# One attention stage for prompt and sample in layer 0, and sample keys transposed by VectorE from a re-laid transfer

## What is computed

```
layer 0:  qa,ka,va (8 heads of 64, forgetting attention), qb,kb,vb (4 heads of 2x64, differential attention)
  prompt: causal attention over its 512 tokens
  sample: for each of 8 requests: K, V = cache[page_table[b]] (1024 x 1024 each) + 8 new rows
          softmax(q K^T * scale + forget sums), differential: p1 - lambda * p2, then P V
          the differential half is RMS-normed over 128 ("subln")
  then w_out, residual, SwiGLU
layer 1:  16 query heads, 4 kv heads of 64; an indexer keeps the top keys of each query
  prompt: attention over the selected keys (a mask)
  sample: for each of 8 requests: K, V = cache[page_table[b]] (1024 x 256 each) + 8 new rows, masked
  then w_out, residual, SwiGLU
```

## Time and profile before

| | us |
|---|---|
| median of 3 runs (2239.94 to 2246.65) | 2245.98 |
| the profiled execution | 2245.45 |
| its span, first to last instruction | 2243.7 |
| layer 0: forget sums | 283 to 298.7 |
| layer 0: prompt attention | 298.7 to 400 |
| layer 0: sample attention, with the prompt's subln | 400 to 631.4 |
| layer 0: the sample's subln | 631.4 to 638.2 |
| layer 1: prompt attention with the top keys | 1426 to 1585.8 |
| layer 1: sample attention | 1585.8 to 1709 |

### The profile page before, as it was taken

The page is one execution under the profiler, slowest core; times in us unless marked ns, Lnnn a source line. Parts: engine busy times, 40 slices in busy tenths (PEclk is TensorE's granted clock), DMA queues, the critical chain, the costliest instruction groups (busy, mean ns, idle before and its releaser), DMA issues. The chain is left out here.

```text
span 2243.7 us, 30894 instructions
## 1 busy us (share of the span) xinstructions
PE 1873.8 (84%) x11782; PEld 1460.6 (65%) x11790; DVE 989.5 (44%) x1686; ACT 569.3 (25%) x1051; POOL 138.0 (6%) x111
## 2 busy tenths in 40 slices
PE   3997678488878999999979768566688899999998
PEld 2765445255556997799767543243445699879986
DVE  3436357644433322232234657999343423132312
ACT  2312135233322321122222222233122322112210
POOL 0423002000000000000001320000000000000000
PEclk9998879799988999999999865688788899999999
DMA  4231100499822231223213300000354222223221
GB/s 151 71 103 47 53 10 1 144 381 344 317 79 66 75 94 66 75 81 88 66 52 114 80 0 4 7 1 1 102 153 113 66 75 75 71 79 86 75 71 57
DMA packets 176270, 201.57 MB, mean 90 GB/s; under 512 B 21290, under 2 KB 130666, under 8 KB 176170
## 3 DMA queue, kind: packets, MB, share of 16 engines
q1 hardware_dynamic: 169176, 193.55, 27.3%
q10 hardware_dynamic: 6914, 6.45, 0.9%
q0 software_dynamic: 80, 0.26, 0.0%
HBM read 191.01 MB, written 9.22 MB: 89 GB/s over the span
## 5 line engine op out<-in xcount | busy, mean ns | idle before, releaser
L206 PE MATMUL ps<-feat_lo,w_hi 128*128 128x288 f32 (+1 forms) x1424 | 422.2, 297 | 15.3 <-PEq L436 8.6
L188 DVE TENSOR_TENSOR w_lo<-w_raw,w_hi 128x2048 fp32r<-128x2048 f32 x97 | 222.4, 2293 | 466.4 <-ACT w_hi L182 466.4
L208 PE MATMUL ps<-feat_hi,w_hi 128*128 128x288 f32 (+1 forms) x1424 | 422.3, 297 | 0.0
L207 PE MATMUL ps<-feat_hi,w_lo 128*128 128x288 f32 (+1 forms) x1424 | 421.9, 296 | 0.0
L182 ACT ACTIVATE w_hi<-w_raw 128x2048 fp32r<-128x2048 f32 x97 | 185.5, 1913 | 448.8 <-PE ps L208 415.4
L206 PEld LDWEIGHTS ps<-feat_lo,w_hi 128*128 128x128 f32 (+1 forms) x1424 | 267.5, 188 | 18.3 <-issue 9.1
L208 PEld LDWEIGHTS ps<-feat_hi,w_hi 128*128 128x128 f32 (+1 forms) x1424 | 267.3, 188 | 1.2
L207 PEld LDWEIGHTS ps<-feat_hi,w_lo 128*128 128x128 f32 (+1 forms) x1424 | 267.4, 188 | 1.1
L206 PE MATMUL ps<-w_lo,feat_hi 128*128 128x512 f32 (+2 forms) x560 | 228.5, 408 | 12.6 <-DVE feat_lo L1439 9.5
L207 PE MATMUL ps<-w_hi,feat_lo 128*128 128x512 f32 (+2 forms) x560 | 223.9, 400 | 0.0
L208 PE MATMUL ps<-w_hi,feat_hi 128*128 128x512 f32 (+2 forms) x560 | 222.9, 398 | 0.0
(11 more groups left out here) (236 smaller groups left out, 2299.1 us busy)
## 6 DMA issues: line engine op xcount, KB each, us to landing
s_kslot<-in_cache_l_k_dram SPq DMA_DIRECT2D x64, 512.0 KB, 7.9
s_vslot<-in_cache_l_v_dram SPq DMA_DIRECT2D x64, 512.0 KB, 7.4
w_raw<-in_w_gate_dram SPq DMA_DIRECT2D x44, 512.0 KB, 4.0
w_raw<-in_w_up_dram SPq DMA_DIRECT2D x44, 512.0 KB, 5.2
w_raw<-in_w_in_dram SPq DMA_DIRECT2D x18, 1024.0 KB, 5.2
w_raw<-in_w_down_dram SPq DMA_DIRECT2D x16, 1024.0 KB, 5.1
s_kslot<-in_cache_l_k_dram SPq DMA_DIRECT2D x64, 128.0 KB, 2.2
s_vslot<-in_cache_l_v_dram SPq DMA_DIRECT2D x64, 128.0 KB, 2.7
```

Of the source, the lines that this page charges most:

```text
L188: dve.tensor_tensor(self.K.w_lo[:, n % 2, :], self.K.w_raw[:, n % 2, :], self.K.w_hi[:, n % 2, :].bitcast(F32), ALU.subtract).then_inc(sel ...
L206: pe.matmul(out, lhs[0], rhs[1], start=start, stop=False)
L207: pe.matmul(out, lhs[1], rhs[0], start=False, stop=False)
L208: return pe.matmul(out, lhs[0], rhs[0], start=False, stop=stop)
```

## The change

- **Layer 0**: prompt attention, sample attention and both sublns become one stage, `attend`. The prompt's units, now in 36 steps (32 units and 4 to drain), are run between the parts of each sample batch: two steps, one, one, and what is left of the batch's share of 4 or 5. The differential pairs come first.
- **Prompt attention** (both layers) is a class, `PromptAttention`. One pair of PSUM banks for scores instead of two, so that scores(u) wait for the exponentials of u-1; one bank for transposed probabilities instead of two; both copies out of it on ScalarE; two buffers of probabilities instead of three. The norms are made once per pair from the sums, not per unit; GpSimd no longer scales.
- **Sample attention** (both layers) is a class, `SampleAttention`, with all 8 batches written out. A page of keys comes in 4 DMAs of 32 partitions each, whose source runs are a quarter row (1 KB in layer 0, 256 bytes in layer 1), and VectorE transposes the page in 32x32 blocks in one instruction of 128 x 1024 (layer 0) or 128 x 256 (layer 1). TensorE's 512 + 128 transposes of keys and their 128 + 32 copies out of PSUM go. Query and probability columns are ordered to suit. The page ids are read once for the keys and again for the values, each just before its page's DMAs.
- Layer 0's key slots are a ring of 4 pages, laid in `resid`, which is loaded again at the end of the stage; the value slots lie in `w_hi` and `w_lo`. Layer 1's are tiles of their own, with 8 pages.
- The first 4 pages of keys and of values of layer 0 are issued in `forget_sums`, ahead of its stores.
- Layer 1 runs `prompt_alone` and then `attend` with no prompt.

The diff, cut to its core:

```diff
 def forget_sums
         @block.sync
         def _(sp):
+            sample.load_k(sp, 0, range(sample.loaded_k))
+            sample.load_v(sp, 0, range(sample.loaded_v))
             sp.wait_ge(S["out"], 1)
...
-def prompt_attention(nc, K, tag, q_at, k_at, v_at, gates, mask, mixed, sample_top=None):
+class PromptAttention:
...
+    def tensor(self, pe, x):
+        def scores(u):
+            if u >= 1:
+                pe.wait_ge(S["exped"], 2 * u)
...
+        def turn(u):
+            for i in self.heads_of(u):
+                if self.mixed(p):
+                    pe.wait_ge(S["blended"], self.n_mixed[u + 1])
+                else:
+                    pe.wait_ge(S["exped"], 2 * u + 1 + i)
+                self.bank_free(pe, ("turn", u, i))
+                for j in range(qt + 1):
+                    ins = pe.transpose(self.T[:, j * P:(j + 1) * P], self.probs[:, u % 2, i, j * P:(j + 1) * P],
+                                       K.c("ident"))
+                ins.then_inc(S["turned"], 1)
...
+        if x < n:
+            scores(x)
+        if 1 <= x <= n:
+            turn(x - 1)
+        if 2 <= x <= n + 1:
+            weigh(x - 2)
...
+    def scalar(self, act, x):
+        if 1 <= x <= n:
+            u = x - 1
+            for i in self.heads_of(u):
+                self.bank_filled(act, ("turn", u, i))
+                if u >= 2:
+                    act.wait_ge(S["weighed"], u - 1)
+                act.activation(self.probs_t[:, u % 2, i, 0:self.width(u)], self.T[:, 0:self.width(u)], ACT.Copy)\
+                   .then_inc(S["t_free"], 1)
+        if x < n:
+            act.wait_ge(S["shifted"], x + 1)
...
-def sample_attention(nc, K, tag, cache_k, cache_v, new_v, row_bias, bias_sel, width, chunks, fill_q, new_k, new_mask,
-                     coef, out, subln=None):
+class SampleAttention:
+    BIAS_AHEAD = N_PAGES // 2
...
+    def load_k(self, sp, b, pages):
+        for j in pages:
+            n = b * N_PAGES + j
+            if j == self.BIAS_AHEAD:
+                if b >= 1:
+                    sp.wait_ge(S["scored"], 3 * b)
+                sp.dma_start(self.bias[:, :], self.row_bias(b)).then_inc(S["bias_in"], 16)
+            if n >= self.ring:
+                sp.wait_ge(S["k_turned"], n - self.ring + 1)
+            page = sp.value_load(self.K.pages[0:1, n:n + 1], min_val=0, max_val=self.cache_k.shape[0] - 1)
+            src = self.cache_k[ds(page, 1), :, :].rearrange("z (c i) (a e) -> z a i c e", c=4, a=4)
+            for a in range(4):
+                dst = self.kslot[32 * a:32 * a + 32, n % self.ring, :].rearrange("i (c e) -> i c e", c=4)
+                sp.dma_start(dst, src[0, a]).then_inc(self.k_in[n % self.ring], 16)
+
+    def load_v(self, sp, b, pages):
+        for j in pages:
+            n = b * N_PAGES + j
+            if j == 0:
+                if b >= 1:
+                    sp.wait_ge(S["weighed"], b)
+                sp.dma_start(self.vnew[:, :], self.new_v(b)).then_inc(S["new_v_in"], 16)
+            page = sp.value_load(self.K.pages[0:1, n:n + 1], min_val=0, max_val=self.cache_v.shape[0] - 1)
+            sp.dma_start(self.vslot[:, j, :], self.cache_v[ds(page, 1), :, :].rearrange("a k d -> (a k) d"))\
+              .then_inc(self.v_in[j], 16)
...
+    def turn_k(self, dve, b, pages):
+        for j in pages:
+            n, g = b * N_PAGES + j, j // 4
+            dve.wait_ge(self.k_in[n % self.ring], 64 * (n // self.ring + 1))
+            if b >= 1:
+                dve.wait_ge(S["scored"], 3 * (b - 1) + 1 + g)
+            src = self.kslot[:, n % self.ring, :].rearrange("p (c b i) -> p c b i", c=4, i=32)
+            dst = self.kt[g][:, :, j % 4 * P:(j % 4 + 1) * P].rearrange("p b (c i) -> p c b i", c=4)
+            dve.transpose(dst, src).then_inc(S["k_turned"], 1)
...
+def attend(nc, K, prompt, sample, subln=None, after=None):
+    def gap(b, g):
+        lo, hi = prompt.steps * b // DEC_BATCH, prompt.steps * (b + 1) // DEC_BATCH
+        cuts = (lo, lo + 2, lo + 3, lo + 4, hi)
+        return range(cuts[g], cuts[g + 1])
...
+        def _(sp):
+            sample.load_k(sp, 0, range(sample.loaded_k, N_PAGES))
+            for b in B:
+                sample.load_v(sp, b, range(sample.loaded_v if b == 0 else 0, N_PAGES))
+                if b + 1 < DEC_BATCH:
+                    sample.load_k(sp, b + 1, range(N_PAGES))
+            if after is not None:
...
+                W.load_up_to(sp, after + 1)
+                sp.dma_start(K.resid[:, 0:PT, :], K.x_prompt[0].rearrange("(t p) d -> p t d", p=P)).then_inc(resid_in, 16)
...
+        def _(pe):
+            for b in B:
+                sample.scores(pe, b)
+                prompt_steps(b, 0)
+                sample.turn_probs(pe, b, 0)
+                prompt_steps(b, 1)
+                sample.turn_probs(pe, b, 1)
+                sample.weigh(pe, b)
+                prompt_steps(b, 2)
+                sample.turn_o(pe, b)
+                prompt_steps(b, 3)
...
+        def _(dve):
+            sample.turn_k(dve, 0, range(N_PAGES))
+            for b in B:
+                sample.shift(dve, s, b)
+                prompt_steps(b, 0)
+                if b + 1 < DEC_BATCH:
+                    sample.queries(dve, s, b + 1)
+                prompt_steps(b, 1)
+                sample.new_probs_out(dve, s, b)
+                if b + 1 < DEC_BATCH:
+                    sample.turn_k(dve, b + 1, range(0, 4))
+                sample.o_out(dve, s, b)
+                prompt_steps(b, 2)
+                if b + 1 < DEC_BATCH:
+                    sample.turn_k(dve, b + 1, range(4, N_PAGES))
+                sample.finish(dve, b)
+                prompt_steps(b, 3)
...
 def two_layers
+            sample.loaded_k, sample.loaded_v = 4, 4
+            forget_sums(nc, K, sample)
...
+            attend(nc, K, prompt, sample, SampleSubln(nc, K, pr, K.c("step")), out0[0][0][0])
...
+            sample.loaded_k, sample.loaded_v = 0, 0
+            attend(nc, K, None, sample)
```

More of the change, by code:

```diff
@@ L169, in load_up_to @@
     def load_up_to(self, sp, last):
-        while self.issued <= min(last, len(self.tiles) - 1):
+        while self.issued <= min(last, self.known() - 1):
             n = self.issued
@@ L816, in turn @@
-            def turn(u):
-                p, qt = units[u]
-                for i in range(1 if mixed(p) else 2):
-                    if mixed(p):
-                        pe.wait_ge(S["blended"], n_mixed[u + 1])
-                    else:
-                        pe.wait_ge(S["exped"], 2 * u + 1 + i)
-                    before = u if i == 0 else n_plain[u]
-                    if before >= 1:
-                        pe.wait_ge(out[i], before)
-                    for j in range(qt + 1):
-                        ins = pe.transpose(K.ps[:, 4 + i, j * P:(j + 1) * P], probs[:, u % 3, i, j * P:(j + 1) * P],
-                                           K.c("ident"))
-                    ins.then_inc(turned[i], 1)
@@ L882, in _ @@
-            for x in range(n + 3):
-                if x < n:
-                    exps(x)
-                if 2 <= x < n + 2:
-                    turn_out(x - 2)
-                if x >= 3:
-                    finish(x - 3)
-        if any(mixed(p) for p in range(PAIRS)):
+            for x in range(prompt.steps):
+                prompt.scalar(act, x)
+        @block.vector
+        def _(dve):
+            s, top = Steps(dve, prompt.S["chain"]), Steps(dve, sample_top.chain)
+            for x in range(prompt.steps):
+                prompt.vector(dve, s, x)
+                for i in range(SampleTop.HALVES * x // prompt.steps, SampleTop.HALVES * (x + 1) // prompt.steps):
+                    sample_top.half(dve, top, i)
@@ L900, in _ @@
         @block.vector
         def _(dve):
-            s = Steps(dve, S["chain"])
-            def top(u):
-                dve.wait_ge(S["scored"], u + 1)
-                a = 2 * (u % 2)
-                dve.tensor_reduce(minus[:, 2 * u:2 * u + 2], K.ps[:, a:a + 2, 0:width(u)], AX, ALU.max, negate=True)\
-                   .then_inc(S["shifted"], 1)
-                if sample_top is not None:
-                    for i in range(SampleTop.HALVES * u // n, SampleTop.HALVES * (u + 1) // n):
-                        sample_top.half(dve, s, i)
@@ L940, in finish @@
-            def finish(u):
-                p, qt = units[u]
-                if not mixed(p) and qt == PT - 1:
-                    dve.wait_ge(S["weighed"], u + 1)
-                    dve.tensor_copy(K.att[:, p, 0:SEQ], O).then_inc(S["chain"], 1)
-                    s.n += 1
-                    s.wait()
-                    dve.tensor_tensor(K.att[:, p, 0:SEQ], K.att[:, p, 0:SEQ], R, ALU.mult).then_inc(S["finished"], 1)
-            top(0)
-            for x in range(n + 3):
-                if x + 1 < n:
-                    top(x + 1)
-                if x >= 3:
-                    finish(x - 3)
-                if x < n:
-                    sums(x)
-                if 2 <= x < n + 2:
```

(19 more changed lines are left out.)

1033 lines of the change are left out of this document (495 added, 538 removed).

## The result

The changed kernel takes 2426.5 us (median of 4 runs, 2423.2 to 2432.1) against 2243.8 (4 runs, 2239.9 to 2246.7): ratio 1.0818, 95% interval 1.079 to 1.0846. It is slower by 183 us; 2432 was predicted. The profiled execution has a span of 2425.0 us against 2243.7. One run further down, the one with early turns, had a lower granted clock in the untouched stages too (0.745 over its span against 0.839 in the changed kernel), so its total is not set against the others.

The account below looks back on a forecast made before the run. Layer 1's sample attention was taken as bound by SyncE issuing, layer 0 by a chain of 41 us a batch. 2245.45 + 2 (layer 0) + 15 (layer 1 prompt) + 170 (layer 1 sample) = 2432 us; range 2320 to 2500.

Parts of the forecast that it names:

- all three terms of the sum: Changes added to the profiled 2245.45 us: +2 layer 0, +15 layer 1's prompt attention, +170 layer 1's sample attention.
- SyncE's issues bound layer 1's sample stage: Layer 1's sample attention: SyncE's issuing sets a batch at 35.6 us, the stage 293 against 123.2, +170.
- The bracket: Layer 1's sample attention: low and high SyncE time per batch, 27.6 to 39.6 us around 35.6.
- The rival of cheap issues: Copies into 32 partitions issue in 0.333 us: layer 1 +106, layer 0 -21, total 2345; chance 0.20.
- Layer 1's prompt stage: Layer 1's prompt attention: 175 us with steps of 5.0 us, +15 (-15 to +40).
- fill, drain and the end of the top keys: Layer 1's prompt attention: 9 us for fill, drain and pair ends, 4 for top keys ending with the last step.
- the closed ring: Layer 1's prompt step: scores(x) wait for the exponentials of x-1, those of x behind both copies of x-1; 5.0 us.
- the chain of a batch: Layer 0, from N to next N: transpose, issues of pages 4 to 7, landing, scores, exponentials, prompt steps; 41 us.
- The predicted +2: Layer 0's attention stage: ends at 640 against 638.2 us, +2 (-45 to +28).
- The tail: Layer 0, behind the last N: weighing 4.3, output, first w_out tile's split, the sample's subln; 12 us.
- The reload of x: End of layer 0's stage: with two w_out tiles issued some 15 us before the last batch ends; uncovered, 12 us.
- N: Layer 0: the point in a batch where VectorE has turned out the new probabilities; batches are counted from N to N.

Follow-up runs that it names:

- early turns: Changed kernel, layer 0: VectorE turns the next batch's first four key pages right after the next queries, ahead of prompt steps; 2523.1 us, period 43.3 us.
- Id reads: Changed kernel, layer 1: a batch's eight page ids read once in a row for keys and values; 2394.0 us, sample stage 227.5 us against 265.2.
- copy count: Changed kernel, layer 1: each key page in one copy of 128 rows instead of four; 2348.7 us, sample stage 199.1 us against 265.2.
- the old function: Changed kernel with layer 1's sample attention and its query and key layout from the kernel before; 2281.3 us, that stage 123.3 us.
- without any copies: Changed kernel, layer 0: no key or value page copied in from the second batch on; 2413.1 us, period 41.9 us.
- the prompt first: Changed kernel, layer 0: all prompt steps run in the first gap of batch 0; 2489.0 us, stage 432.6 us.

## Why the prediction was right

The total was 6 us off and its sign and main term were right, but all three terms of the sum were off in size, and two of them rested on a wrong mechanism.

- **SyncE's issues bound layer 1's sample stage: right.** Id reads, copy count and the old function each moved the stage as that says, and SyncE waited 0.5 us. The sizes were high: a copy's pitch is 0.50 us, not 0.60, and an id read 0.58, not 0.75. Batch 31.6 instead of 35.6, the stage +142 instead of +170. The bracket (27.6 to 39.6) held both. The pieces give 8 x 2.58 + 8 x 1.09 + 2 x 0.74 = 30.8 (the bias and vnew at 0.74 each by the timeline above). Most of what is left are the rare long issues: by the key copies alone, 4.4 us over seven batches.
- **The rival of cheap issues was half right:** the instruction is 0.317, like those into 128 partitions, but a written-out copy has two register steps before it, so the pitch is no 0.43.
- **Layer 1's prompt stage: near in size (+21 for +15), the wrong term.** I took the step as 5.0 us before and after and put the growth into fill, drain and the end of the top keys (9 + 4). The 5.0 of before was the whole stage over 32 and held the ends too; the step was 4.58 there and is 5.24 now, and the ends are about as long as they were (18 and 19 us). So the closed ring itself cost 20 us, and that the terms of the ends gave nearly as much was luck. Nor had I counted the clock: 0.73 after, 0.80 before, with TensorE's busy time at 121 us instead of 108 for the same instructions.
- **Layer 0: near in size, wrong in cause.** The step that failed is "VectorE transposes page 0 and so frees a ring slot; SyncE issues pages 4 to 7; the last copy lands", taken as the chain of a batch. SyncE does wait 83.5 us for the turns, but without any copies the period is 41.9, and with early turns 43.3. What remains is TensorE's own list: the prompt's steps and the sample's pieces stand in one in-order queue, and TensorE is busy 260 of 355.6 us at a clock of 0.72 (264 of 332.7 at 0.88 and 0.92 before). A batch has 230.9 / 7 = 33.0 us of it, where the prediction put some 25. (The chain's terms add up to 36.6 and 42.2, not 36.7 and 42.3, which changes nothing.) That these waits in line, with the lower clock, are what makes up the 41.9 was argued from what the two runs leave over; no run opened the rings in layer 0, since all eight banks are in use there.
- **Where layer 0's gain went.** By the run with the prompt first: the new pieces one behind the other take 432.6 us, the old ones 339.5, so the pieces became 93 us longer (steps of 4.9 us for units of 101.3 / 32 = 3.2, and batches of 31.3, the length of SyncE's list, where the reciprocals of the kernel before stand (621.6 - 456.2) / 7 = 23.6 apart); laying them together gives 77 back. +16 is what is left. The predicted +2 came out as +24 with the forget sums.
- **The tail** was 17 us, not 12. The reload of x was covered, as predicted; the last weighing, at a granted clock of 0.63, ended 8.5 us behind N and not 4.3.
- **Not foreseen: -10 us ahead of the forget sums.** The first w_out copy is issued at 624.4 instead of 220.2, so the projection and the forget gates have less beside them (218.0 to 213.0 and 20.3 to 16.5 us). The diff shows the move, and no term of the sum stood for it. That this is the cause was not tried by itself.

That the sum came out within 6 us is in part luck: +170 was 28 too high, and layer 0 (22), layer 1's prompt (6) and the -10 nearly made up for it: -28 + 22 + 6 - 10 and +4 in the untouched stages give -6.

## What to carry to other kernels

Before a transfer is cut into more pieces, count what its queue issues per iteration: here a copy had a pitch of 0.5 us and a page id read in between cost 0.58, so that 24 more copies and 8 more reads, some 17 us a batch, replaced 16 TensorE transposes a batch that were busy 3 us in layer 1 before. When two stages are laid into one, the pieces that share PSUM can lose their double buffers, as here; run the parts one behind the other to see what the sharing costs and what the overlap gives, since both can be large and cancel (93 and 77 us here). A run with the transfers left out tells at once whether a wait seen in SyncE's queue sets a period or only fills it.

## What the runs showed that was not expected

- A copy into 32 partitions issues in 0.317 us, one into 128 in 0.333, while those into 64 partitions in the earlier trace rows take 0.61: the issue time did not follow the number of partitions.
- An id read costs about the same between the copies of pages as in a row (0.57 and 0.55 us; its load is 0.267 in the median). Loads of 0.44 to 0.63 stand right behind the copies of the bias and of the new values and at the end of SyncE's waits, one or two in a batch; the 0.547 of the earlier trace rows was such a one and not the usual price between issues.
- A few key issues take 1.0 to 1.9 us with no wait shown.
- The same 696 matmuls of one stage were busy 95 to 121 us, in profiles with granted clocks from 0.85 to 0.73 for that stage.
- Layer 0's loop, with the same code in eight kernels, had periods from 42.9 to 45.3 us in single executions. A difference of 1 or 2 us a batch between two of them is read only where TensorE's busy time and clock agree.
